# Norms ahead of two feed-forwards: halves made from x itself, the row factor applied in PSUM

## The reference, cut to what matters

```python
for i in range(DEPTH):                                  # "nsa", "swa"
    h = rms_norm(x, norm_mix[i])
    x = x + mixer(h, ...)                               # ends in the output projection w_o
    h = rms_norm(x, norm_ffn[i])                        # x * rsqrt(mean(x*x) + eps) * gain
    x = x + conv_ffn(h, ffn_w_gu[i], ffn_conv_w[i], ffn_conv_b[i], ffn_w_down[i])

def conv_ffn(h, w_gu, conv_w, conv_b, w_down):
    gate, up = split(h @ w_gu)
    gate = causal_conv_of_width_3(gate) + conv_b        # over positions
    return (silu(gate) * up) @ w_down
```

## Time and profile before

| | us |
|---|---|
| median of 3 runs | 2662.39 |
| lowest and highest | 2658.5, 2663.87 |
| profiled execution | 2661.52 |
| its span | 2659.7 |
| PE busy | 2541.7 (96%) |
| POOL busy | 1789.8 (67%) |
| DVE busy | 1278.4 (48%) |
| ACT busy | 790.5 (30%) |
| mean granted clock of PE | 0.984 of full |

### The profile page before, as it was taken

One profiled execution on the slowest core, in us unless ns is written; L12 is line 12 of the kernel. 1 busy time (PEld: TensorE's weight loads), 2 busy tenths in 40 slices (PEclk: granted clock), 3 DMA queues, 4 the chain that ended last, 5 costly groups with the idle time before them and its releaser, 6 DMA issues.

```text
span 2659.7 us, 34453 instructions
## 1 busy us (share of the span) xinstructions
PE 2541.7 (96%) x12236; PEld 2129.4 (80%) x12236; DVE 1278.4 (48%) x1927; ACT 790.5 (30%) x1687; POOL 1789.8 (67%) x1580
## 2 busy tenths in 40 slices
PE   7889989999999899999999979999998999999998
PEld 5678878888888788888888867888887887788886
DVE  7967755333027753332168876333116445533312
ACT  2256652111006821110046642111005554211101
POOL 6757667666667776666678867666665567666663
PEclk9899999999999999999999999999999999999999
DMA  3210012223221022223221212222221112222222
GB/s 132 87 56 17 17 40 87 95 95 97 100 79 56 33 87 95 95 95 104 90 72 64 72 40 72 95 100 97 95 87 59 63 64 71 72 95 100 97 95 71
DMA packets 58119, 208.65 MB, mean 78 GB/s; under 512 B 6496, under 2 KB 6752, under 8 KB 58016
## 3 DMA queue, kind: packets, MB, share of 16 engines
q1 hardware_dynamic: 57744, 206.88, 23.4%
q10 hardware_dynamic: 272, 0.39, 0.0%
HBM read 205.09 MB, written 2.16 MB: 78 GB/s over the span
## 4 chain that ended last, share of the span: by engine, by line
PE 76%; DVE 13%; POOL 5%; ACT 4%; issue 2%; DMA 1%; SPq 0%; ACTq 0%; DVEq 0%; POOLq 0%
PE PS L796 22%; PE PS L798 22%; PE PS L797 22%; POOL WL L559 2%; DVE BLK L2128 2%; PE PS L829 1%; ACT GP L1550 1%; DVE GTL L2233 1%; DVE PC L2414 1%; POOL WH L557 1%; PE PS L976 1%; DVE RD L2469 1%; ACT MP L1770 1%; DVE NM L2176 1%; PE PS L1175 1%
## 5 line engine op out<-in xcount | busy, mean ns | idle before, releaser
L559 POOL TENSOR_TENSOR WL<-raw,WH 128x1024 fp32r<-128x1024 f32 x380 | 920.0, 2421 | 31.7
L796 PE MATMUL PS<-HH,WH 128*128 128x512 f32 x2272 | 901.7, 397 | 34.4 <-POOL HL L719 11.5
L798 PE MATMUL PS<-HH,WL 128*128 128x512 f32 x2272 | 891.2, 392 | 0.0
L797 PE MATMUL PS<-HL,WH 128*128 128x512 f32 x2272 | 891.0, 392 | 0.0
L796 PEld LDWEIGHTS PS<-HH,WH 128*128 128x128 f32 x2272 | 431.1, 190 | 134.2 <-issue 15.5
L798 PEld LDWEIGHTS PS<-HH,WL 128*128 128x128 f32 x2272 | 430.1, 189 | 91.9
L797 PEld LDWEIGHTS PS<-HL,WH 128*128 128x128 f32 x2272 | 431.3, 190 | 86.4
L556 POOL TENSOR_TENSOR WH<-raw,SC 128x32 fp32r<-128x32 f32 x380 | 117.4, 309 | 501.6 <-DMA raw<-stream 490.0
L557 POOL TENSOR_SCALAR WH<-raw 128x992 fp32r<-128x992 f32 x380 | 405.2, 1066 | 0.0
L796 PE MATMUL PS<-GH,WH 128*128 (+1 forms) x704 | 273.9, 389 | 0.0
L797 PE MATMUL PS<-GL,WH 128*128 (+1 forms) x704 | 273.9, 389 | 0.0
(11 more groups left out here) (348 smaller groups left out, 3568.9 us busy)
## 6 DMA issues: line engine op xcount, KB each, us to landing
raw<-stream SPq DMA_DIRECT2D x380, 512.0 KB, 3.3
X<-x SPq DMA_DIRECT2D x4, 512.0 KB, 5.4
out<-X SPq DMA_DIRECT2D x8, 256.0 KB, 2.0
PR<-params SPq DMA_DIRECT2D x1, 536.0 KB, 7.5
spare_raw_nsa<-stream SPq DMA_DIRECT2D x1, 512.0 KB, 3.3
spare_raw_swa<-stream SPq DMA_DIRECT2D x1, 512.0 KB, 4.5
spare_raw_diff<-stream SPq DMA_DIRECT2D x1, 512.0 KB, 4.6
spare_raw_fox<-stream SPq DMA_DIRECT2D x1, 512.0 KB, 4.0
```

Source lines behind the costliest of these rows:

```text
L559: pool.tensor_tensor(WL[:, w], raw[:, w], hi.bitcast(F32), ALU.subtract).then_inc(chunk_split, 1)
L796: pe.matmul(to, h, his[k], start=start and k == 0, stop=False)
L797: pe.matmul(to, h, los[k], start=False, stop=False)
L798: last = pe.matmul(to, l, his[k], start=False, stop=stop and k == n_k - 1)
```

## The change

For the norms k = 1 and k = 3 (LATE) the halves are made of x times the gain alone, without the factor of the row. Output tile 7 is made tile by tile of h, each signalling h_free, and ACT writes HH of x over the tile of HH that has just been used (`late_hi`); DVE writes HL (`late_lo`), tiles 0 to 6 before the residual of tile 7, and the last one behind it. POOL's `norm_lo` for these norms is gone. PE starts gate and up with these halves, makes the sums behind `first_two` (`late_sums`), and the broadcast behind the tiles of f=1 (`late_scale`, bank 5); the filler of these norms is gone. DVE copies the broadcast to RB in SBUF and multiplies each gate and up tile by it in place in PSUM (signal `rescaled`), before ACT and DVE go on with it as before. Output tiles 6 and 7 go to banks 4 and 5, so the wait for x_updated is left out there.

```diff
--- before.py
+++ after.py
@@ -84,6 +84,14 @@
          ("final", FINAL, None),
          ("ln", LN1G, LN1B), ("ln", LN2G, LN2B), ("ln", LN1G + 1, LN1B + 1), ("ln", LN2G + 1, LN2B + 1)]
 
+LATE = (1, 3)
+
+
+def whole_norms(k):
+
+    return k - sum(x < k for x in LATE)
+
+
 C_COS, C_SIN, C_ID, C_DIAG, C_PREV, C_CMP = 0, S, 2 * S, 2 * S + P, 2 * S + 2 * P, 2 * S + 3 * P
 CONST_N = 2 * S + 4 * P
 
@@ -168,7 +176,7 @@
 
 def out_bank(kind, t):
 
-    return (proj_bank(t + 1) if kind == "nsa" else proj_bank(t)) if t < 2 else (0, 1, 3, 2, 0, 1)[t - 2]
+    return (proj_bank(t + 1) if kind == "nsa" else proj_bank(t)) if t < 2 else ((0, 1, 3, 2, 4, 5) if kind in GROUPED else (0, 1, 3, 2, 0, 1))[t - 2]
 
 
 def bank_at(kind, part, y=0):
@@ -330,6 +338,9 @@
             spare[kind] = (at(f"spare_raw_{kind}", low, CW), at(f"spare_high_{kind}", high, CW, F32R),
                            at(f"spare_low_{kind}", low, CW, F32R))
 
+        RB = at("RB", 102400, S)
+        assert base + 102400 + S * 4 <= nc.sbuf_usable_end and level + 2 * FT * S * 4 <= 102400
+
         PS = ctx.enter_context(nc.psum_tensor("PS", [P, 8, S], F32))
 
 
@@ -365,6 +376,7 @@
         centred = sem("centred")
         scaled_x = sem("scaled_x")
         normed = sem("normed")
+        h_free = sem("h_free")
         h_hi = sem("h_hi")
         h_lo = [sem("h_lo_even"), sem("h_lo_odd")]
         gate_act = sem("gate_act")
@@ -433,6 +445,7 @@
         post_root = sem("post_root")
         post_inverse = sem("post_inverse")
         post_out = sem("post_out")
+        rescaled = sem("rescaled")
         conv_first = sem("conv_first")
         conv_done = sem("conv_done")
         silu_done = sem("silu_done")
@@ -771,7 +784,6 @@
                 split_spare(n, kind)
                 out_rest(7)
                 split(q["out_chunk"] + SPARE_TILE, q["gu_chunk"] + 3)
-                norm_lo(2 * n + 1)
 
             done = 0
             for n, q in enumerate(layers):
@@ -858,6 +870,21 @@
                 pe.matmul(PS[:, 3], ONE_F[:], WK[:, 5], start=True, stop=True).then_inc(scale_ready, 1)
                 if 0 < k < 8:
                     keep_busy(0, 18 if ln else 12)
+
+            def late_sums(k):
+
+                pe.wait_ge(added, (KT - 2) * (k + 1))
+                for b in range(QT):
+                    pe.matmul(PS[:, 4 + b, 0:1], WK[:, 4, b * P:(b + 1) * P], ONE_F[:, 0:1], start=True, stop=False)
+                pe.wait_ge(squared, KT * (k + 1))
+                for b in range(QT):
+                    last = pe.matmul(PS[:, 4 + b, 0:1], WK[:, 1, b * P:(b + 1) * P], ONE_F[:, 0:1], start=False, stop=True)
+                last.then_inc(summed, 1)
+
+            def late_scale(k):
+
+                pe.wait_ge(diag_ready, k + 1)
+                pe.matmul(PS[:, 5], ONE_F[:], WK[:, 5], start=True, stop=True).then_inc(scale_ready, 1)
 
             def grouped(n, q, k_norm):
                 kind, c0, nsa = q["kind"], q["proj_chunk"], q["kind"] == "nsa"
@@ -1325,13 +1352,20 @@
                 c = q["out_chunk"] - 1
                 for t in range(SPARE_TILE + 1, OUT_TILES):
 
-                    if t >= 6:
+                    if t >= 6 and q["kind"] in MERGED:
                         pe.wait_ge(x_updated, 2 * KT * n + t - 3)
                     pe.wait_ge(chunk_split, c + t + 1)
-                    products((c + t) % SLOTS, PS[:, out_bank(q["kind"], t)], h_his, h_los).then_inc(chunk_used, 1)
+                    if t == OUT_TILES - 1 and q["kind"] in GROUPED:
+                        for k in range(KT):
+                            last = products((c + t) % SLOTS, PS[:, out_bank(q["kind"], t)], [h_his[k]], [h_los[k]], 1,
+                                            k == 0, k == KT - 1, k)
+                            last.then_inc(chunk_used if k == KT - 1 else h_free, 1)
+                    else:
+                        products((c + t) % SLOTS, PS[:, out_bank(q["kind"], t)], h_his, h_los).then_inc(chunk_used, 1)
 
             def feed_forward(n, q):
                 c = q["gu_chunk"]
+                late = 2 * n + 1 in LATE
 
                 def pair(f, i, j):
 
@@ -1344,13 +1378,19 @@
                 if n:
 
                     pe.wait_ge(gated, n * FT - 1)
+                if late:
+                    pe.wait_ge(x_updated, 2 * KT * n + 4)
                 first_two(c, h_wait(2 * n + 1))
 
                 if n:
                     pe.wait_ge(gated, n * FT)
+                if late:
+                    late_sums(2 * n + 1)
                 for y in range(2, 4):
                     pe.wait_ge(chunk_split, c + y + 1)
                     products((c + y) % SLOTS, PS[:, y], h_his, h_los).then_inc(chunk_used, 1)
+                if late:
+                    late_scale(2 * n + 1)
                 with pe.Fori(0, FT // 2 - 1) as i:
                     pair(2, i, 0)
                     pair(3, i, 1)
@@ -1408,7 +1448,8 @@
                 else:
                     grouped(n, q, kn)
                 out_project(n, q)
-                norm(kn + 1)
+                if kn + 1 not in LATE:
+                    norm(kn + 1)
                 feed_forward(n, q)
             norm(8)
 
@@ -1416,17 +1457,30 @@
         @block.scalar
         def _(act):
             own = Steps(act, act_step)
+
+            def late_hi(k, t):
+
+                if t < KT - 1:
+                    act.wait_ge(h_free, (KT - 1) * LATE.index(k) + t + 1)
+                else:
+                    act.wait_ge(chunk_used, layers[k // 2]["gu_chunk"])
+                act.activation(tile(HH, t), tile(X, t), ACT.Copy, scale=param("norms", NORMS[k][1] * KT + t)).then_inc(h_hi, 1)
 
             def norm(k):
                 kind, gain, bias = NORMS[k]
                 act.preload_act_table(ACT.Sqrt)
                 for t in range(KT):
+                    if k in LATE and t == KT - 1:
+                        for h in range(KT - 1):
+                            late_hi(k, h)
                     if k == 0:
                         act.wait_ge(x_landed[t // 2], 16)
                     else:
                         act.wait_ge(x_updated, KT * (k - 1) + t + 1)
                     if t >= 2:
                         act.wait_ge(added, (KT - 2) * k + max(t - 2, 1))
+                    if k in LATE and t == KT - 1:
+                        late_hi(k, t)
                     act.activation(WK[:, t % 2], tile(X, t), ACT.Square).then_inc(squared, 1)
                 if kind == "ln":
                     act.wait_ge(variances, k - 4)
@@ -1436,6 +1490,9 @@
                     act.activation(ST[:, 0], PS[:, 4:8, 0], ACT.Sqrt, bias=SC[:, SC_EPS:SC_EPS + 1], scale=1.0 / D
                                    ).then_inc(rooted, 1)
 
+                if k in LATE:
+                    return
+
                 def hi(t):
                     if k == 8:
                         return
@@ -1444,7 +1501,7 @@
                     act.activation(tile(HH, t), normalised(k, t), ACT.Copy).then_inc(h_hi, 1)
 
                 for t in range(KT):
-                    act.wait_ge(scaled_x, KT * k + t + 1)
+                    act.wait_ge(scaled_x, KT * whole_norms(k) + t + 1)
                     if kind == "ln":
                         act.activation(tile(X, t), WK[:, t % 4], ACT.Identity, scale=param("norms", gain * KT + t),
                                        bias=param("norms", bias * KT + t)).then_inc(normed, 1)
@@ -1928,7 +1985,10 @@
                 with act.Fori(0, FT // 2) as i:
                     for y in range(2):
                         f = i * 2 + y
-                        act.wait_ge(chunk_used, i * 4 + (c + 2 * y + 1))
+                        if 2 * n + 1 in LATE:
+                            act.wait_ge(rescaled, i * 4 + (2 * n * FT + 2 * y + 1))
+                        else:
+                            act.wait_ge(chunk_used, i * 4 + (c + 2 * y + 1))
                         cw = f * 4 + 4 * FT * n
 
                         act.activation(WK[:, y], PS[:, 2 * y], ACT.Identity, scale=param("conv", cw + 2),
@@ -2013,6 +2073,10 @@
                 dve.wait_ge(rooted, k + 1)
                 own.link(dve.reciprocal(ST[:, 1], ST[:, 0]))
                 diagonals(WK[:, 5], ST[:, 1]).then_inc(diag_ready, 1)
+                if k in LATE:
+                    dve.wait_ge(scale_ready, k + 1)
+                    own.link(dve.tensor_copy(RB[:], PS[:, 5]))
+                    return
 
                 def lo(t):
 
@@ -2517,11 +2581,22 @@
                                                     op0=ALU.mult, op1=ALU.add)
                 return dve.tensor_tensor(tile(X, t), tile(X, t), PS[:, bank], ALU.add)
 
+            def late_lo(k, t):
+
+                dve.wait_ge(h_hi, KT * k + t + 1)
+                dve.scalar_tensor_tensor(out=tile(HL, t), in0=tile(X, t), scalar=param("norms", NORMS[k][1] * KT + t),
+                                         in1=tile(HH, t).bitcast(F32), op0=ALU.mult, op1=ALU.subtract
+                                         ).then_inc(h_lo[t % 2], 1)
+
```

(12 more changed lines are left out.)

## The result

The changed kernel takes 2668.96 us in the median of 20 runs (2664.43 to 2673.97), the kernel before, run beside it, 2660.36 us (2656.7 to 2664.07). The ratio is 1.0032 with a 95% interval of 1.0026 to 1.0038: slower by 8.6 us, clear of noise. The forecast was +6.2 us, 2667.7.

The account below looks back on a forecast made before the run. TensorE, busy 96% of a 2659.7 us span, was taken as the bound. Per norm, 1.6 us (-8.69 + 1.70 + 5.50 + 3.1) plus 1.5 of clock, twice, gave +6.2 on 2661.5: 2667.7 us, range 2660.5 to 2671.5.

Parts of the forecast that it names:

- leaves the path: Stretch from the output projection's last product to gate and up's first: 8.69 us per norm removed.
- sums: The 16 small matmuls, moved behind the first two gate and up tiles: 1.70 us per norm on PE.
- late_lo (first two tiles over 10.88): DVE's HL instructions alternate with POOL's, holding PE in the first two tiles: 3.1 us per norm, between 0.5 and 4.5.
- broadcast to first product: Chain from broadcast through copy, rescale, ACT and two conv steps before f=2: 5.50 us per norm, bounds 5.3 to 5.7.
- clock: PE idles about 4.3 us behind the broadcast, so its clock halves: 1.5 us per norm, bounds 0 and 1.7.
- The rival in which DVE keeps the pair: late_lo follow each other without waiting for POOL: 0.5 us per norm, not 3.1; total 2659.5 to 2662.5; chance 0.18.
- The sum of ten terms: Ten parts of the chain from broadcast to first product of f=2, adding to 5.50 us per norm.
- The term with no row, DVE writing PSUM: Rescale of gate in PSUM, within the chain behind the broadcast: taken as 0.69 us, bounded by 0.6 and 0.75.
- The rival of a second fall, at the sums: The sums' small matmuls after held tiles lower the clock again: further 1.5 us per norm, 2670.7; chance 0.11.
- The filler costs nothing.: In the old norm stretch, filler matmuls add no time, because the chain and not PE sets its length.
- Edits with no price: Banks 4 and 5, per-tile h_free and loop rescales cost PE nothing; DVE rises from 4.4 to 5.8 us per f.
- Slower by more than 0.2%: Outcome class for the whole kernel, chance 0.42, against 0.54 for within and 0.04 for faster.

Follow-up runs that it names:

- the kernel where POOL waits: Changed kernel with POOL splitting the third gate and up chunk only after HL of tile 6 is made; 2666.14 us, ratio 1.0015 to the kernel before.
- The filler experiment: Changed kernel plus 24 filler matmuls of 384 columns behind the broadcast of each late norm; 2663.78 us, ratio 1.0012 to the kernel before.

## Why the prediction was right, and where it was not

The direction and the mechanism held: slower, by late_lo behind POOL, by the chain behind the broadcast and by the clock. 2668.96 lies in the range, 1.3 us above the forecast; part of that closeness is luck, since the kernel before came out at 2660.36 and not at the 2661.5 that the forecast starts from, and the loss is 8.6 us against 6.2. Per term and norm:

| term, us | forecast | nsa | swa |
|---|---|---|---|
| leaves the path | -8.69 | -8.69 | -8.69 |
| sums | 1.70 | 1.70 | 1.70 |
| late_lo (first two tiles over 10.88) | 3.1 | 2.98 | 3.05 |
| broadcast to first product | 5.50 | 5.59 | 5.57 |
| clock | 1.5 | 2.4 | 1.7 |
| sum | 3.1 | 4.0 | 3.3 |

For "swa" the products of the output projection are issued by 970.59, the first two tiles end at 984.52, the broadcast starts at 997.23 and the first product at 1002.80; the entries for "nsa" are from rows shown. The two sums are 7.3 us. The other 1.3 us of the measured 8.6 have no place in these rows; the interval of the ratio alone is 1.6 us to either side.

**The late_lo.** Right almost to the row: held at tiles 0, 3, 6 and 7, and seven instructions beside POOL's in turn. The row that decided it was the one of eight DVE instructions that alternate with POOL. The rival in which DVE keeps the pair fell: each POOL instruction beside the seven is 0.3 to 0.5 us longer, which is one wait and not seven, so the waiting engine gets the pair each time. The rule of the Trainium skill (SBUF — State Buffer, "SBUF: two separate sides") that the pair is held exclusively for one instruction agrees with 12.68 us beside POOL against 6.87 us in the kernel where POOL waits; the order of the two in waiting is what these runs add.

**The chain.** Right. The sum of ten terms gave 5.50, the trace 5.59 and 5.57. The term with no row, DVE writing PSUM, was estimated at 0.69 and two of them take 1.30 us in one row:

```profile
445.07 1.30 DVE L2625 TENSOR_TENSOR PS<-PS,RB 128x512 f32<-128x512 f32 x2 [0.23 <-DVE RB L2078]
```

**The clock.** The fall came in both norms as forecast, but 1.5 us was too little: this is the term of the sum that was mis-sized. I had taken the lower level for some 3.0 us of products, from the earlier trace rows; the slow products lasted 5.1 us in the first norm and 3.7 us in the second, and the loss is 2.4 and 1.7 us. The bounds, 0 and 1.7, took it that what falls into the idle time is saved; in the first norm the clock was down for 1.9 us of the hole and the loss was the larger one. The second stretch of the earlier trace rows also ends at 1565.50 by the choice of the stretch and not by the clock: the products go on 0.43 us apart until 1566.06. With the losses of the trace the sum is +7.3 in place of +6.2, so this term carries 1.1 of the 2.4 us between the forecast and the measurement. The filler experiment gives 2.6 per norm, by which it would carry nearly all; its interval is too wide to say so. The rival of a second fall, at the sums, did not come: the granted clock is 1.00 from 416.55 to 443.

**"The filler costs nothing."** Wrong. It did no harm to the forecast, since the 8.69 us that leave the path were measured with the filler in. But the sentence that "the chain and not PE sets its length" fails for the 1.2 us by which the first 12 matmuls delay the sums; without them the chain to be removed is 7.47 us. A reader who had compared the end of the last square (415.56 + 0.63 = 416.19) with the start of the first sums (416.75) would have seen that PE, and not the square, was the last to be ready.

**Edits with no price.** Right for the loop: PE stays full with two rescales and with four. The rescales themselves did not wait for POOL, 0.68 to 0.70 us each, as said. But DVE's turn per f was put at 5.8 us and is 7.0 (47.55 of 74 us), because GL, which the change moves and does not touch, now meets POOL. It was overlooked, and had no price only since DVE has time to spare there. The banks and h_free show no cost in the trace: the products of output tile 7 are issued every 0.23 us to the end.

**The chances.** "Slower by more than 0.2%" had 0.42 and "no change" 0.54, since the forecast lay on the limit. With the clock term as in the trace it would have lain at 2668.8, 1.1 us further to the slow side.

## What to carry to other kernels

Before a step is moved off the path, follow what its result now has to go through and where the next wait on that stands: a factor applied after the product is still a chain, and here it cost its whole length with its broadcast right ahead of the first wait on it, and only the 0.9 us of the broadcast one tile earlier. Work handed to DVE in a stretch where POOL streams should be counted at one instruction of DVE per instruction of POOL, if DVE's instruction reads two tensors from SBUF. POOL's need not read two: L570 reads one, and beside late_lo it took 1.48 us in place of 1.02 like the others. And an instruction that the change only moves can come to meet POOL, as GL did. Filler that holds the clock is worth it only where PE would wait anyway; ahead of a step that others wait for, it should be no longer than that wait. How little of it still holds the clock is another matter: with 4 in place of 12 matmuls the clock fell in one of two norms.

## What the runs showed of the hardware that I had not expected

After the hole of 4.58 us the lower clock lasted through 5.1 us of products in one norm, although it had begun 1.9 us before the end of the hole. After one of 4.55 us it began only some 0.4 us behind the hole, and the slow products took 3.7 us. The price of a hole of one length is not one number, and one execution does not give it. And a filler of 2.10 us that replaced a wait of 0.66 us cost 1.2 us per norm, while taking all filler out cost 2.2 us of clock in the same place, so that the two kernels differ by 0.0002 in the ratio, with 0.0008 expected of these two numbers and an interval that reaches to 0.0010, and look alike in time, though their traces do not.
